# Neighbourhood attention of the first block, two heads at a time on the two halves of TensorE's array

## The chip, the cores and the metric

The kernel runs on one core of one Trainium2 chip. The metric is the device time of one execution in microseconds (us). All data is float32. The engines are called by the names of the profile: PE is TensorE's matmul, PEld its weight load, DVE is VectorE, ACT is ScalarE, POOL is GpSimd, SP is SyncE, which issues the loads of the weights.

## What is computed

The reference is a model of two blocks with two layers each, over 256 tokens of 1,024 features. The change touches one part of the first block, its neighbourhood attention. In each of the two layers it takes 8 heads of 64 features:

```python
mix-in of a layer of the first block (cut):
    proj = h @ w_in[i] + b_in[i]
    qkv = proj[..., 2 * CONV_CH:].reshape(B, T, 3, N_HEADS, HEAD_DIM)
    conv_out = conformer_conv(a, g, conv_w[i], ...)
    attn_out = neighbourhood_attention(q, k, v, rpb[i])   # softmax(q k / 8 + bias + window mask) v
    mix = jnp.concatenate([conv_out, attn_out], axis=-1) @ w_out[i] + b_out[i]
```

The kernel computes the scores of a head over all 256 keys; what lies outside the window is masked by the table `relb`, which holds the relative bias and the mask together.

## The kernel before

Every engine has a program of its own, written out by hand, and waits on semaphores. In layer `l` of the first block PE does, in this order: the projection, three units of `conditions(l)`, the norm of the convolution, the attention, the output product `block1_out`, and then the feed-forward part. In layer 0 the attention lies at 117 to 160 us of the span, in layer 1 at 567 to 611 us.

**The filler.** `conditions(l)` computes a product that only the second block needs. It is a generator of 13 units, numbered from 0. Unit u of PE multiplies one weight tile (`row`, 16 matmul instructions in four column quarters of 32) into bank 1, and then folds the row of unit u-1 (`fold`, 4 instructions of two columns). Unit 12 only folds. ACT has a generator of its own, which copies bank 1 to `cond_row` (L1088), one copy for each unit. Bank 1 is single: PE's `fill` lets row u start only when ACT has copied row u-1. Three units are done ahead of the norm; the attention asks for the rest, one at the head of each of its rounds, on PE and on ACT.

**The attention.** One head to a round, over `i`, as a pipeline. In round i

- PE does a filler unit; the scores of head i, into bank 2 or 3 (two products of 64 rows by 128 columns, four instructions); the transposes of head i-2 (four, L485), which wait for `nbr_prob`; and the product with v of head i-3 (two products with 64 output columns, four instructions), which waits for `nbr_turned`.
- ACT does a filler copy; the copy of the transposed head i-3 (L1124); the two exponentials of head i (L1130), which wait for `nbr_max`; and in every second round the copy of a finished pair of heads to `mix1` (L1136).
- DVE normalises head i-2 (reciprocal L1474, two multiplications L1476), and then adds the bias to the scores of head i (L1485) and takes the negated row maximum (L1488).

Probabilities have three buffers (`prob1[:, i % 3]`), their transposes two (`pt1`). All matmuls issued through the helper `mm` have line L377.

The loads of weights are issued by SP into a ring of six slots, each as soon as the unit that held the slot has been used. POOL loads `relb` for layer 1 when the last scores of layer 0 have been read (`nbr_scored`).

Of the kernel before, what the change touches and what calls it, by code (L numbers as in the profile page):

```python
# [8 lines left out]
ALU = mybir.AluOpType  # L9
ACT = mybir.ActivationFunctionType  # L10
AX = mybir.AxisListType


P = 128
T = 256
TT = T // P
# [4 lines left out]
CC = CONV_CH // P  # L21
# [137 lines left out]
def build(nc, weights, params, consts, x_t, ctx_t, p_t, rel, out):  # L159
    with ExitStack() as ctx:  # L160
# [14 lines left out]
        def carver(space, limit):  # L175
            at = [0]

            def carve(*shape):
                n = int(np.prod(shape))
                v = space[:, at[0]:at[0] + n]  # L180
                at[0] += n
                assert at[0] <= limit, at[0]
                names = "abcd"[:len(shape)]
                if len(shape) > 1:
                    v = v.rearrange(f"p ({' '.join(names)}) -> p {' '.join(names)}",
                                    **{k: s for k, s in zip(names[1:], shape[1:])})
                return v
            return carve
# [12 lines left out]
        gi, gf, lf, labs = cut(4, 8), cut(4, 8), cut(4, 8), cut(4, 8)  # L201


        cut = carver(work, WORK)
        cen, sq = cut(KC, T), cut(KC, T)
        res, mix1, ple = cut(KC, T), cut(KC, T), cut(KC, T)
# [8 lines left out]
        std1, rstd1, sig_sb = cut(T), cut(T), cut(2, T)  # L215
        cond_s = cut(KC, 32)

        gcmp, geq = (act_sb[:, i, 0, 0:TT * 64].rearrange("p (a b) -> p a b", b=64) for i in range(2))


        MIX, GLU, PROB, TAIL = 6144, 12288, 21624, 29048
        extra = [work[:, at:at + UC] for at in (0, UC, MIX, GLU, GLU + UC, PROB)]

        def slot_view(slot):
# [125 lines left out]
        def _(eng):  # L350
# [5 lines left out]
            def fill(key, bank, read_by):  # L356

                if readers[bank] is not None:
                    eng.wait_ge(*readers[bank])
                count[bank] += 1  # L360
                placed[key] = (bank, count[bank])
                readers[bank] = read_by
                return ps[:, bank, :]
# [12 lines left out]
            def mm(o, lhs, rhs, start, stop, **kw):  # L376
                ins = eng.matmul(o, lhs, rhs, start=start, stop=stop, **kw)  # L377
                if release[0]:
                    ins.then_inc(s["weights_used"], int(release[0]))
                    release[0] = 0  # L380
                return ins
# [84 lines left out]
            def block1_attention(l, filler):  # L466
                eng.wait_ge(s["qk_out"], CC * (l + 1))
                eng.wait_ge(s["v_out"], 2 * (l + 1))
                for i in range(HEADS + 3):
                    next(filler, None)  # L470
                    if i < HEADS:
                        b, p0 = 2 + i % 2, DH * (i % 2)
                        o = fill(("s", l, i), b, (s["nbr_scored"], HEADS * l + i + 1))
                        for t in range(TT):
                            last = mm(o[:, t * T:(t + 1) * T], q1[p0:p0 + DH, i // 2, t * P:t * P + P],
                                      k1[p0:p0 + DH, i // 2, :], True, True)
                        last.then_inc(bank_full[b], 1)
                    if 2 <= i < HEADS + 2:
                        h = i - 2
                        b = 4 + h % 2  # L480
                        eng.wait_ge(s["nbr_prob"], HEADS * l + h + 1)
                        o = fill(("pt", l, h), b, (s["nbr_turned"], HEADS * l + h + 1))
                        for t in range(TT):
                            for kt in range(TT):
                                last = eng.transpose(o[:, kt * T + t * P:kt * T + t * P + P],  # L485
                                                     prob1[:, h % 3, t, kt * P:kt * P + P], ident)
                        last.then_inc(bank_full[b], 1)
                    if i >= 3:
                        h = i - 3
                        eng.wait_ge(s["nbr_turned"], HEADS * l + h + 1)  # L490
                        if h % 2 == 0:
                            o2 = fill(("o", l, h // 2), 6 + (h // 2) % 2, (s["nbr_out"], CC * l + h // 2 + 1))
                        for kt in range(TT):
                            last = mm(o2[DH * (h % 2):DH * (h % 2) + DH, 0:T],
                                      v1[:, kt, h * DH:h * DH + DH], pt1[:, h % 2, kt, :], kt == 0, kt == TT - 1)
                        if h % 2 == 1:
                            last.then_inc(bank_full[6 + (h // 2) % 2], 1)

            def block1_out(l):
                eng.wait_ge(s["conv_mixed"], CC * (l + 1))  # L500
# [517 lines left out]
        def tile(eng, *key):  # L1018

            b, n = placed[key]  # L1020
            eng.wait_ge(bank_full[b], n)
            return ps[:, b, :]
# [28 lines left out]
        @block.gpsimd  # L1051
        def _(eng):

            eng.wait_ge(s["late_loaded"], 16 * N_LATE)
            for l in range(DEPTH):
                if l:
                    eng.wait_ge(s["nbr_scored"], HEADS * l)
                for r in range(ROWS):
                    p0 = GRID_W * (r % 2)
                    src = rel[l, :, :, ROWS - 1 - r:2 * ROWS - 1 - r, :].rearrange("c h i j -> c h (i j)")  # L1060
                    eng.dma_start(relb[p0:p0 + GRID_W, r // 2, :, :], src).then_inc(s["rel_loaded"], 16)
                eng.wait_ge(s["rel_loaded"], 16 * ROWS * (l + 1))
                for t in range(TT):
                    mask = con[:, CN("nbr_mask", t * T, T)].unsqueeze(1).broadcast_to([P, HEADS, T])
                    eng.tensor_tensor(relb[:, t], relb[:, t], mask, ALU.add).then_inc(s["rel_ready"], 1)
# [3 lines left out]
        def _(eng):  # L1069
# [47 lines left out]
                                   scale=par[:, PC(f"conv_ln_g{l}", j)]).then_inc(s["conv_mixed"], 1)  # L1117

            def block1_attention(l, filler):
                for i in range(HEADS + 4):  # L1120
                    next(filler, None)
                    if 3 <= i < HEADS + 3:
                        o = tile(eng, "pt", l, i - 3)
                        eng.activation(pt1[:, (i - 3) % 2].rearrange("p a b -> p (a b)"), o, ACT.Copy)\  # L1124
                            .then_inc(s["nbr_turned"], 1)
                    if i < HEADS:
                        k = HEADS * l + i + 1
                        eng.wait_ge(s["nbr_max"], k)
                        for t in range(TT):
                            eng.activation(prob1[:, i % 3, t, :], prob1[:, i % 3, t, :], ACT.Exp,  # L1130
                                           bias=rmax[:, i % 3, t:t + 1], accum_out=rsum[:, i % 3, t:t + 1])\
                                .then_inc(s["nbr_exp"], 1)
                    if i >= 5 and i % 2 == 1:
                        h2 = (i - 5) // 2
                        o = tile(eng, "o", l, h2)
                        eng.activation(mix1[:, CC + h2, :], o[:, 0:T], ACT.Copy).then_inc(s["nbr_out"], 1)  # L1136

            def block1_out(l):
                for c in range(KC):
# [240 lines left out]
        def _(eng):  # L1380
            order = [0]

            def link(ins):

                order[0] += 1
                ins.then_inc(s["dve_order"], 1)
                eng.wait_ge(s["dve_order"], order[0])
# [79 lines left out]

            def block1_attention(l):
                eng.wait_ge(s["rel_ready"], TT * (l + 1))
                for i in range(HEADS + 2):  # L1470
                    if i >= 2:
                        h = i - 2
                        eng.wait_ge(s["nbr_exp"], 2 * (HEADS * l + h + 1))
                        link(eng.reciprocal(rinv[:, h % 3, :], rsum[:, h % 3, :]))  # L1474
                        for t in range(TT):
                            ins = eng.tensor_scalar(prob1[:, h % 3, t, :], prob1[:, h % 3, t, :],  # L1476
                                                    rinv[:, h % 3, t:t + 1], None, ALU.mult)
                        ins.then_inc(s["nbr_prob"], 1)
                    if i < HEADS:
                        k = HEADS * l + i + 1  # L1480
                        pr = prob1[:, i % 3]
                        o = tile(eng, "s", l, i)
                        if i >= 3:
                            tile(eng, "pt", l, i - 3)
                        eng.tensor_tensor(pr, o.rearrange("p (a b) -> p a b", b=T), relb[:, :, i, :], ALU.add)\  # L1485
                            .then_inc(s["nbr_scored"], 1)
                        eng.wait_ge(s["nbr_scored"], k)
                        eng.tensor_reduce(rmax[:, i % 3, :], pr, AX.X, ALU.max, negate=True).then_inc(s["nbr_max"], 1)  # L1488

            def block1_out(l):  # L1490
                for c in range(KC):
# [705 lines left out]
```

## Time and profile before

| | |
|---|---|
| median of 3 runs | 2448.18 us (2445.6 to 2450.01) |
| the profiled execution's own time | 2445.93 us |
| its span in the profile | 2444.1 us |
| PE busy | 2205.6 us, 90% of the span |
| DVE busy | 691.0 us, 28% |
| ACT busy | 369.2 us, 15% |
| mean granted clock of TensorE | 0.949 of full speed |

The span is the time from the first to the last instruction in the trace; the remaining 1.8 us lie around it. Busy shares are averages over the whole program, which has stages with quite different limits; the 40 slices of the page are 61 us each, so that the attention of layer 0 is spread over the second and the third of them.

### The profile page before, as it was taken

Reading aid. Unit: us, or ns where it says so; the run is one execution under the profiler, and the core shown is the slowest. Engines: PE = TensorE matmul, PEld = TensorE weight load, DVE = VectorE, ACT = ScalarE, POOL = GpSimd, SP = SyncE. Lnnn points to the kernel's source line nnn. Section 1 sums busy time; section 2 is a strip of 40 time slices with the busy share of each in tenths; the row PEclk is TensorE's granted clock in tenths of the full one; section 3 lists DMA queues with packets and bytes.
Section 4 is the critical chain, followed back from the end, with each engine's and each line's share of the span. In section 5 each row is a group of like instructions: output and inputs, shape, how many; then the busy total and the mean of one; then the engine's idle time right before and its main releaser. Section 6 shows DMA issues by size and latency. Waiting matters only on the chain.

```text
span 2444.1 us, 34578 instructions
## 1 busy us (share of the span) xinstructions
PE 2205.6 (90%) x14880; PEld 1533.5 (63%) x14880; DVE 691.0 (28%) x1680; ACT 369.2 (15%) x894; POOL 24.3 (1%) x16
## 2 busy tenths in 40 slices
PE   7799999998899999999999999889986778998766
PEld 6668888785776566666666666437464454486455
DVE  2932000265311111111111111224027663232754
ACT  1132000104210000000000000120124230112331
POOL 1010000000000000000000000000000000000000
PEclk9999999998899999999999999999998889998778
DMA  8463444245249999999999999602210001122000
GB/s 291 155 225 128 148 154 155 104 155 207 69 170 420 420 420 421 420 420 420 420 421 420 420 416 417 266 35 86 86 52 1 1 1 69 69 104 86 0 1 17
DMA packets 71930, 506.59 MB, mean 207 GB/s; under 512 B 7776, under 2 KB 9824, under 8 KB 11232
## 3 DMA queue, kind: packets, MB, share of 16 engines
q1 hardware_dynamic: 69296, 497.18, 51.3%
q0 software_dynamic: 1152, 4.19, 0.7%
q8 instruction: 120, 1.97, 0.3%
q10 hardware_dynamic: 1328, 2.97, 0.3%
q14 instruction: 34, 0.28, 0.0%
HBM read 503.27 MB, written 1.05 MB: 206 GB/s over the span
## 4 chain that ended last, share of the span: by engine, by line
PE 56%; DMA 10%; DVE 7%; ACT 2%; issue 1%; SPq 0%; DVEq 0%; ACTq 0%
PE ps L377 54%; DMA ring<-weights 9%; DMA work<-weights 1%; PE ps L931 1%; DVE small L1941 1%; ACT work L1278 1%; DVE work L1406 1%; DVE work L1936 1%; DVE work L1858 0%; PE ps L603 0%; DVE work L1811 0%; DVE work L1802 0%; DVE work L1410 0%; DVE work L1906 0%; DVE work L1844 0%
## 5 line engine op out<-in xcount | busy, mean ns | idle before, releaser
L377 PE MATMUL ps<-work 128*32 128x256 f32 (+6 forms) x5464 | 569.1, 398 | 52.0 <-DMA ring<-weights 15.3
L377 PE MATMUL ps<-work,ring 128*128 128x256 f32 (+1 forms) x2048 | 575.8, 442 | 25.8 <-DVE work L1722 12.1
L377 PE MATMUL ps<-xc,ring 128*128 128x256 f32 x2368 | 520.6, 381 | 8.2 <-DVE xc L1418 7.1
L377 PEld LDWEIGHTS ps<-work,ring 128*128 128x128 f32 x2048 | 391.3, 192 | 206.1 <-issue 150.3
L377 PEld LDWEIGHTS ps<-xc,ring 128*128 128x128 f32 x2368 | 450.8, 191 | 82.3 <-DMA ring<-weights 11.3
L377 PEld LDWEIGHTS ps<-work 128*32 128x32 f32 (+3 forms) x5464 | 325.9, 127 | 228.5 <-issue 135.1
L377 PE MATMUL ps<-ring,work 128*32 128x256 f32 (+3 forms) x3832 | 407.0, 437 | 8.5 <-ACT work L1088 6.5
L377 PEld LDWEIGHTS ps<-ring,work 128*32 128x32 f32 (+1 forms) x3832 | 224.2, 123 | 141.9 <-issue 91.1
L1612 DVE TENSOR_TENSOR work<-work,ps 128x256 f32<-128x256 f32 x42 | 17.7, 421 | 455.0 <-ACT work L1182 455.0
L377 PE MATMUL ps<-work,con 128*128 128x256 f32 (+1 forms) x278 | 95.6, 497 | 41.3 <-DVE work L1444 13.7
L1182 ACT ACTIVATE work<-ps 128x256 f32<-128x256 f32 x42 | 16.1, 384 | 638.1 <-PE ps L377 638.1
L377 PEld LDWEIGHTS ps<-work,con 128*128 128x128 f32 x278 | 58.5, 218 | 69.1 <-issue 55.4
L1444 DVE SCALAR_TENSOR_TENSOR work<-work,par 128x256 f32<-128x256 f32 x240 | 95.2, 478 | 0.0
L931 PE MATMUL ps<-con,work 128*128 128x128 f32 x160 | 32.8, 329 | 55.3 <-ACT work L1327 54.4
L1597 DVE TENSOR_TENSOR work<-ps,work 128x512 f32<-128x512 f32 x68 | 47.1, 692 | 99.2 <-PE ps L377 99.0
L931 PEld LDWEIGHTS ps<-con,work 128*128 128x128 f32 x160 | 20.2, 163 | 85.0 <-issue 57.3
L1693 DVE TENSOR_TENSOR work<-work,ps 128x256 f32<-128x256 f32 x22 | 9.3, 421 | 205.9 <-ACT work L1220 205.9
L1764 DVE TENSOR_TENSOR work<-ps,con 128x256 f32<-128x256 f32 x10 | 4.2, 424 | 190.1 <-PE ps L377 189.9
L1220 ACT ACTIVATE work<-ps 128x256 f32<-128x256 f32 x22 | 8.4, 384 | 207.7 <-PE ps L377 207.7
L1334 ACT ACTIVATE small<-par,small 128x1 f32<-128x1 f32 x48 | 14.1, 294 | 166.0 <-DVE small L1942 165.9
L1750 DVE SCALAR_TENSOR_TENSOR work<-work,par 128x512 f32<-128x512 f32 (+1 forms) x64 | 38.8, 680 | 0.0
L1626 DVE TENSOR_TENSOR work<-work 128x512 f32<-128x512 f32 x14 | 9.7, 692 | 98.9 <-ACT work L1188 98.9
(218 smaller groups left out, 1129.8 us busy)
## 6 DMA issues: line engine op xcount, KB each, us to landing
ring<-weights SPq DMA_DIRECT2D x303, 1024.0 KB, 17.5
work<-weights SPq DMA_DIRECT2D x168, 1024.0 KB, 22.0
work<-rel POOLq DMA_DIRECT2D x8, 512.0 KB, 11.4
con<-consts ACTq DMA_DIRECT2D x1, 1368.0 KB, 10.2
xc<-x_t SPq DMA_DIRECT2D x1, 1024.0 KB, 7.5
xc<-ctx_t ACTq DMA_DIRECT2D x1, 1024.0 KB, 21.5
out<-work SPq DMA_DIRECT2D x1, 1024.0 KB, 3.9
par<-params SPq DMA_DIRECT2D x1, 872.0 KB, 9.0
```

Of the source, the lines that this page charges most:

```text
L377: ins = eng.matmul(o, lhs, rhs, start=start, stop=stop, **kw)
L931: last = eng.transpose(o[:, kt * P:kt * P + P], prob2[:, k % 4, kt * P:kt * P + P], ident)
L1182: eng.activation(pair_s[:, n % 2, :], o[:, 0:GW], ACT.Silu).then_inc(s["pair_silu"], 1)
L1278: ins = eng.activation(decay[:, n, :], amask[:, n, :], ACT.Exp, bias=nm_row[:, n:n + 1])
L1334: eng.activation(esink[:, k % 4, :], par[:, PC(f"sink{l}", h)], ACT.Exp, bias=rmax[:, k % 4, 0:1])
L1406: link(eng.reciprocal(rstd[:, 0:n], std[:, 0:n]))
L1444: ins = eng.scalar_tensor_tensor(out=conv_acc[:, j, :], in0=src, scalar=w, in1=conv_acc[:, j, :], op0=ALU.mult, op1=ALU.add)
L1597: return eng.tensor_tensor(r, o.rearrange("p (a b) -> p a b", b=T), r, ALU.add)
L1612: eng.tensor_tensor(pair_a[:, n % 2, :], pair_s[:, n % 2, :], o[:, GW:2 * GW], ALU.mult)\
L1750: ins = eng.scalar_tensor_tensor(out=acc, in0=src, scalar=w, in1=acc, op0=ALU.mult, op1=ALU.add)
L1936: eng.tensor_tensor(pr, o, con[:, CN("win_mask", qt * 2 * T, 2 * T)], ALU.add)\
L1941: link(eng.tensor_reduce(rmax[:, k % 4, 0:1], pr, AX.X, ALU.max, negate=True))
```

## The change

The attention goes over pairs of heads, `CC` = 4 rounds of scores in place of 8. A head of the pair has rows 0 to 63 of the array and the other rows 64 to 127 in the scores, which go to banks 2 and 3 and are issued in turns; in the product with v the two heads have columns 0 to 63 and 64 to 127, and are issued in turns too. Round i of PE is now: a filler unit, the transposes of pair i-2, the scores of pair i, another filler unit, the product with v of pair i-3. ACT's round: a filler copy, the copies of the transposed pair i-2, four exponentials, another filler copy, the copy of a finished pair to `mix1`. DVE normalises pair i-1 (one reciprocal of 4 columns, four multiplications) and then does one addition and one maximum over 1,024 columns for pair i. Probabilities have two buffers of a pair, transposes as well; the latter lie over `act_sb` and `silu_sb`, which the feed-forward part uses.

```diff
+        prob_pairs = work[:, PROB:PROB + 4 * TT * T].rearrange("p (a b c) -> p a b c", b=TT, c=T)
+        turned_pairs = work[:, ACT_AT:ACT_AT + 4 * TT * T].rearrange("p (a b c) -> p a b c", b=TT, c=T)
...
-                for i in range(HEADS + 3):
+                for i in range(CC + 3):
                     next(filler, None)
...
+                    if 2 <= i < CC + 2:
+                        k = CC * l + i - 1
+                        eng.wait_ge(s["nbr_prob"], k)
+                        for half in range(2):
+                            o = fill(("pt", l, i - 2, half), 4 + half, (s["nbr_turned"], 2 * k - 1 + half))
+                            for t in range(TT):
+                                for kt in range(TT):
+                                    last = eng.transpose(o[:, kt * T + t * P:kt * T + t * P + P],
+                                                         prob_pairs[:, 2 * (i % 2) + half, t, kt * P:kt * P + P], ident)
+                            last.then_inc(bank_full[4 + half], 1)
+                    if i < CC:
+                        both = [fill(("s", l, i, half), 2 + half, (s["nbr_scored"], CC * l + i + 1)) for half in range(2)]
                         for t in range(TT):
...
+                            for half in range(2):
+                                p0 = DH * half
+                                last = mm(both[half][:, t * T:(t + 1) * T], q1[p0:p0 + DH, i, t * P:t * P + P],
+                                          k1[p0:p0 + DH, i, :], True, True)
+                                if t == TT - 1:
+                                    last.then_inc(bank_full[2 + half], 1)
+                    next(filler, None)
                     if i >= 3:
...
+                        c = i - 3
+                        eng.wait_ge(s["nbr_turned"], 2 * (CC * l + c + 1))
+                        o2 = fill(("o", l, c), 6 + c % 2, (s["nbr_out"], CC * l + c + 1))
                         for kt in range(TT):
...
+                            for half in range(2):
+                                h = 2 * c + half
+                                last = mm(o2[DH * half:DH * half + DH, 0:T], v1[:, kt, h * DH:h * DH + DH],
+                                          turned_pairs[:, 2 * (c % 2) + half, kt, :], kt == 0, kt == TT - 1)
+                        last.then_inc(bank_full[6 + c % 2], 1)
...
             def block1_attention(l, filler):
-                for i in range(HEADS + 4):
+                for i in range(CC + 4):
                     next(filler, None)
...
+                    if 2 <= i < CC + 2:
+                        for half in range(2):
+                            o = tile(eng, "pt", l, i - 2, half)
+                            eng.activation(turned_pairs[:, 2 * (i % 2) + half].rearrange("p a b -> p (a b)"), o, ACT.Copy)\
+                                .then_inc(s["nbr_turned"], 1)
+                    if i < CC:
+                        eng.wait_ge(s["nbr_max"], CC * l + i + 1)
+                        for half in range(2):
+                            n = 2 * (i % 2) + half
+                            for t in range(TT):
+                                eng.activation(prob_pairs[:, n, t, :], prob_pairs[:, n, t, :], ACT.Exp,
+                                               bias=rmax[:, n, t:t + 1], accum_out=rsum[:, n, t:t + 1])\
+                                    .then_inc(s["nbr_exp"], 1)
+                    next(filler, None)
+                    if i >= 4:
+                        o = tile(eng, "o", l, i - 4)
+                        eng.activation(mix1[:, CC + i - 4, :], o[:, 0:T], ACT.Copy).then_inc(s["nbr_out"], 1)
...
+                for i in range(CC + 1):
+                    if i >= 1:
...
+                        eng.wait_ge(s["nbr_exp"], 4 * k)
+                        link(eng.reciprocal(rinv[:, slots, :], rsum[:, slots, :]))
+                        for n in range(slots.start, slots.stop):
+                            for t in range(TT):
+                                ins = eng.tensor_scalar(prob_pairs[:, n, t, :], prob_pairs[:, n, t, :],
+                                                        rinv[:, n, t:t + 1], None, ALU.mult)
                         ins.then_inc(s["nbr_prob"], 1)
...
+                        eng.tensor_tensor(pr, ps[:, 2:4, :].rearrange("p a (b c) -> p a b c", c=T),
+                                          relb[:, :, 2 * i:2 * i + 2, :].rearrange("p b a c -> p a b c"), ALU.add)\
                             .then_inc(s["nbr_scored"], 1)
                         eng.wait_ge(s["nbr_scored"], k)
...
+                        eng.tensor_reduce(rmax[:, slots, :], pr, AX.X, ALU.max, negate=True).then_inc(s["nbr_max"], 1)
```

## Rows read from the trace of the kernel before

**Rows 1.** The page: span, busy share and granted clock in 40 slices

```profile
span 2444.1 us, 34578 instructions
...
PE   7799999998899999999999999889986778998766
...
PEclk9999999998899999999999999999998889998778
```

**Rows 2.** Windows of the two attention stages, layer 0 and layer 1

```profile
core 0: us, PE busy (x) PEld busy (x) DVE busy (x) ACT busy (x) POOL busy (x), PEclk, DMA share, GB/s
116.87:160.28 43.41, 40.05 (x281) 23.55 (x280) 19.96 (x46) 22.42 (x61) 2.76 (x4) 0.88 0.66 226
566.92:611.19 44.27, 41.31 (x282) 24.08 (x281) 19.92 (x46) 22.16 (x60) 0.00 (x0) 0.84 0.57 214
```

**Rows 3.** Timeline of PE, layer 1, one head's round: start, us, instructions

```profile
587.91 1.07 PE L377 MATMUL ps<-ring,work 128*32 128x256 f32 x16
588.91 0.61 PE L377 MATMUL ps<-con,work 128*128 128x2 f32 x4
589.45 1.13 PE L377 MATMUL ps<-work 64*128 64x256 f32 x4
590.50 0.66 PE L485 MATMUL ps<-con,work 128*128 128x128 f32 x4
591.09 1.08 PE L377 MATMUL ps<-work 128*64 128x256 f32 x4
592.10 1.07 PE L377 MATMUL ps<-ring,work 128*32 128x256 f32 x16
```

**Rows 4.** Timeline of PE near the start of both stages, with waits

```profile
122.38 1.07 PE L377 MATMUL ps<-ring,work 128*32 128x256 f32 x16 [2.85 <-ACT work L1088]
...
572.26 1.94 PE L377 MATMUL ps<-ring,work 128*32 128x256 f32 x16 [2.41 <-ACT work L1088]
...
575.08 2.07 PE L377 MATMUL ps<-work 64*128 64x256 f32 x4
577.08 1.93 PE L377 MATMUL ps<-ring,work 128*32 128x256 f32 x16
...
581.88 1.12 PE L485 MATMUL ps<-con,work 128*128 128x128 f32 x4
582.93 1.86 PE L377 MATMUL ps<-ring,work 128*32 128x256 f32 x16
```

**Rows 5.** Timeline of ACT, start of the stage in layer 1

```profile
571.76 0.36 ACT L1088 ACTIVATE work<-ps 128x256 f32<-128x256 f32 x1
572.14 1.28 ACT L1130 ACT_TABLE_LOAD   x1
573.43 0.51 ACT L1130 ACTIVATE work<-work,small 128x256 f32<-128x256 f32 x1
...
573.94 0.49 ACT L1130 ACTIVATE work<-work,small 128x256 f32<-128x256 f32 x1
...
574.43 0.36 ACT L1088 ACTIVATE work<-ps 128x256 f32<-128x256 f32 x1
```

**Rows 6.** Timeline of DVE, layer 1

```profile
570.67 0.69 DVE L1485 TENSOR_TENSOR work<-ps,work 128x512 f32<-128x512 f32 x1
...
590.61 0.69 DVE L1485 TENSOR_TENSOR work<-ps,work 128x512 f32<-128x512 f32 x1 [2.05 <-PE ps L377]
591.34 0.69 DVE L1488 TENSOR_REDUCE small<-work 128x2 f32<-128x512 f32 x1
...
592.13 0.62 DVE L1476 TENSOR_SCALAR work<-work,small 128x256 f32<-128x256 f32 x2
```

**Rows 7.** Groups by shape, DVE: busy us, mean ns

```profile
L1802 DVE TENSOR_REDUCE work<-ps 128x8 f32<-128x1024 f32 x8 | 9.8, 1225 | 13.2 <-PE ps L377 13.2
```

**Rows 8.** Windows around changes of the granted clock, columns as in rows 2

```profile
122.10:123.80 1.70, 1.42 (x20) 0.92 (x20) 0.09 (x1) 1.67 (x3) 0.00 (x0) 1.00 0.00 0
123.80:125.50 1.70, 1.70 (x6) 1.33 (x5) 0.00 (x0) 1.11 (x5) 0.00 (x0) 0.50 0.69 212
132.30:134.00 1.70, 1.70 (x18) 0.66 (x10) 0.70 (x4) 1.25 (x5) 0.00 (x0) 0.50 0.17 19
570.10:571.80 1.70, 0.00 (x0) 0.00 (x0) 1.67 (x4) 1.70 (x5) 0.00 (x0) 0.75 1.06 443
583.70:585.40 1.70, 1.70 (x17) 0.86 (x10) 0.43 (x2) 1.36 (x6) 0.00 (x0) 0.74 0.21 63
```

**Rows 9.** Timeline of PE, last products with v in both layers

```profile
157.96 1.83 PE L377 MATMUL ps<-work 128*64 128x256 f32 x8
...
608.84 1.83 PE L377 MATMUL ps<-work 128*64 128x256 f32 x8
```

More of the change, by code:

```diff
@@ L201, in build @@
         gi, gf, lf, labs = cut(4, 8), cut(4, 8), cut(4, 8), cut(4, 8)
+        MIX, GLU, PROB, ACT_AT, TAIL = 6144, 12288, 21624, 25208, 29048
         cut = carver(work, WORK)
@@ L216, in build @@
         cond_s = cut(KC, 32)
+        prob_pairs = work[:, PROB:PROB + 4 * TT * T].rearrange("p (a b c) -> p a b c", b=TT, c=T)
+        turned_pairs = work[:, ACT_AT:ACT_AT + 4 * TT * T].rearrange("p (a b c) -> p a b c", b=TT, c=T)
         gcmp, geq = (act_sb[:, i, 0, 0:TT * 64].rearrange("p (a b) -> p a b", b=64) for i in range(2))
-        MIX, GLU, PROB, TAIL = 6144, 12288, 21624, 29048
         extra = [work[:, at:at + UC] for at in (0, UC, MIX, GLU, GLU + UC, PROB)]
@@ L468, in block1_attention @@
                 eng.wait_ge(s["v_out"], 2 * (l + 1))
-                for i in range(HEADS + 3):
+                for i in range(CC + 3):
                     next(filler, None)
-                    if i < HEADS:
-                        b, p0 = 2 + i % 2, DH * (i % 2)
-                        o = fill(("s", l, i), b, (s["nbr_scored"], HEADS * l + i + 1))
-                        for t in range(TT):
[L475 to L487, printed above, removed]
@@ L488, in block1_attention @@
+                    next(filler, None)
                     if i >= 3:
[L489 to L492, printed above, removed]
+                        c = i - 3
+                        eng.wait_ge(s["nbr_turned"], 2 * (CC * l + c + 1))
+                        o2 = fill(("o", l, c), 6 + c % 2, (s["nbr_out"], CC * l + c + 1))
@@ L493, in block1_attention @@
                         for kt in range(TT):
[L494 to L497, printed above, removed]
+                            for half in range(2):
+                                h = 2 * c + half
+                                last = mm(o2[DH * half:DH * half + DH, 0:T], v1[:, kt, h * DH:h * DH + DH],
+                                          turned_pairs[:, 2 * (c % 2) + half, kt, :], kt == 0, kt == TT - 1)
@@ L1056, in _ @@
                 if l:
-                    eng.wait_ge(s["nbr_scored"], HEADS * l)
+                    eng.wait_ge(s["nbr_scored"], CC * l)
                 for r in range(ROWS):
@@ L1119, in block1_attention @@
             def block1_attention(l, filler):
-                for i in range(HEADS + 4):
+                for i in range(CC + 4):
                     next(filler, None)
[L1122 to L1136, printed above, removed]
+                    if 2 <= i < CC + 2:
[15 more added lines that the diff above has]
+                        eng.activation(mix1[:, CC + i - 4, :], o[:, 0:T], ACT.Copy).then_inc(s["nbr_out"], 1)
             def block1_out(l):
@@ L1469, in block1_attention @@
                 eng.wait_ge(s["rel_ready"], TT * (l + 1))
[L1470 to L1477, printed above, removed]
-                        ins.then_inc(s["nbr_prob"], 1)
[L1479 to L1485, printed above, removed]
+                for i in range(CC + 1):
+                    if i >= 1:
+                        k = CC * l + i
+                        slots = slice(2 * ((i - 1) % 2), 2 * ((i - 1) % 2) + 2)
+                        eng.wait_ge(s["nbr_exp"], 4 * k)
[4 more added lines that the diff above has]
+                                                        rinv[:, n, t:t + 1], None, ALU.mult)
+                        ins.then_inc(s["nbr_prob"], 1)
+                    if i < CC:
+                        k = CC * l + i + 1
+                        slots = slice(2 * (i % 2), 2 * (i % 2) + 2)
+                        pr = prob_pairs[:, slots]
+                        for half in range(2):
+                            tile(eng, "s", l, i, half)
+                            if i >= 2:
+                                tile(eng, "pt", l, i - 2, half)
+                        eng.tensor_tensor(pr, ps[:, 2:4, :].rearrange("p a (b c) -> p a b c", c=T),
+                                          relb[:, :, 2 * i:2 * i + 2, :].rearrange("p b a c -> p a b c"), ALU.add)\
@@ L1486, in block1_attention @@
                             .then_inc(s["nbr_scored"], 1)
                         eng.wait_ge(s["nbr_scored"], k)
-                        eng.tensor_reduce(rmax[:, i % 3, :], pr, AX.X, ALU.max, negate=True).then_inc(s["nbr_max"], 1)
+                        eng.tensor_reduce(rmax[:, slots, :], pr, AX.X, ALU.max, negate=True).then_inc(s["nbr_max"], 1)
             def block1_out(l):
```

## The prediction, made before the changed kernel was run

> **What bounds the kernel now.** I read the page first: PE is busy nine tenths of most slices at nine tenths of its clock [rows 1], so time is won or lost where PE's own sequence is longer or shorter. Then the windows of the two stages that the change touches: 43.4 and 44.3 us, PE busy in 40 and 41 of them, DVE in 20 and ACT in 22, the DMA engines at 0.66 and 0.57 [rows 2]. All that can move is inside 88 us of 2,444.
>
> Then PE's timeline. A head's round is one unbroken run of PE: row and fold 1.54 us (587.91 to 589.45), scores 1.05, transposes 0.59, product with v 1.01, together 4.19 [rows 3]. So here PE is the bound, in most rounds. What the reader should see besides is the exception at the start of both stages: PE stands 2.85 and 2.41 us before a row, released by ACT's filler copy L1088 [rows 4]. Bank 1 is single, so each row waits for the copy of the row before it. In the present order this copy stands at the head of ACT's round, ahead of the exponentials that depend on PE, and is early except at the start, where ACT is late with other work.
>
> Last the clock. It is 1.00 until 123.80 and 0.50 after it, until 134.0; in layer 1 it is 0.50 from about 571 to about 584.7 [rows 8]. Half is 1.2 GHz, full 2.4. Both falls come with or just after the standing time of rows 4; both returns come only after more than 10 us in which PE had nearly no gap. At half clock row and fold take 2.82 us (572.26 to 575.08), scores 2.00, four transposes 1.05 [rows 4].
>
> **What the change takes away.** Scores: eight instructions per pair, issued in turns on two row halves. No row here shows row halves at work; the nearest is the filler row, where instructions on four column quarters go 16 to 1.00 us, 62 ns each, against 252 ns each for the product with v, alone on its 64 columns [rows 3]. So quarters run side by side. By that row two halves do as well: scores of a pair 1.05 us in place of 2.10. Upper bound: no overlap, 2.10. Product with v: column halves, the same kind as the row: 1.0 in place of 2.0, upper bound 2.0. Transposes and fillers: as many as before. PE's work falls by 2.06 us for each of 8 pairs, 16.5 us in all.
>
> The Trainium skill (TensorE: Matmul & The Clock Gate, Part 3) says that matmuls on different row groups run concurrently; by it the lower value holds for the scores too, and the sum is the same.
>
> **What it adds.** DVE: addition and maximum over 1,024 columns. The nearest row is 1.225 us for a reduction of that width [rows 7]; two of the present size would be 1.38. I take 1.25 start to start. ACT: four exponentials in place of two; one with its accumulator read takes 0.51 start to start [rows 5], four 2.1. DVE's four multiplications are 1.2 (two are 0.62 [rows 6]) with a reciprocal before. None of this fills an engine: 4 us of DVE and about 4.5 of ACT in a round of 8.
>
> But one part of the order is new. ACT's second filler copy of round i stands **behind** the four exponentials of pair i, and PE's first row of round i+1 waits for that copy. The exponentials wait for the maximum, this for the addition, this for the scores of pair i, and these come on PE after the first filler and the transposes of the same round. That is a closed loop through PE, DVE and ACT, once per round. From the end of the scores: hand-over 0.05, addition 1.25, maximum 1.26 with its hand-over, exponentials 2.1, copy and hand-over to PE 0.6 (the copy starts at 571.76, the row at 572.26 [rows 4, 5], and I add 0.1). In all 5.26 us. In it PE has the second filler, 1.54, and in round 3 also the product with v, 1.0; then it stands for 3.7 us (2.7 in round 3). Queued behind it are transposes and scores of the next round, and so DVE's addition and ACT's exponentials.
>
> **The schedule at full clock.** Round 0 of layer 1: DVE can add at 570.67 as now [rows 6], maximum ready at 573.2, table loaded at 573.42 [rows 5], exponentials done 575.5, row 5 of the filler at 576.05, where it now starts at 577.08 [rows 4]. Round 1 (no transposes): 1.54 + 1.05 + 5.26 = 7.85. Rounds 2 and 3: 1.54 + 1.18 + 1.05 + 5.26 = 9.03 each; two heads now take 8.38. Round 4 to 6, no more exponentials: filler 1.54, transposes 1.18, last fold 0.54, product 1.0, transposes 1.18, then two copies of ACT, 1.35 with hand-over, beside the next product, last product 1.0: 7.8. Sum 33.7 after 576.05: 609.75, against 610.67 (608.84 + 1.83 [rows 9]). Layer 0, from 122.38 [rows 4] with the same 3.79 to the next row: 159.88, against 159.79 [rows 9]. Together -0.8 us: the 16.5 us of PE's work become standing time of PE, and nothing is won.
>
> **The clock.** At half clock round 1 has 1.28 more for the filler and 0.95 more for the scores, 2.2; rounds 2 and 3 have 0.92 more for eight transposes too, 3.15 each. That is 8.5 per layer. The loop through DVE and ACT does not shrink in return. In the present kernel gaps of 2.4 and 2.85 us, one in a stage, went with a fall [rows 4, 8]; now there are four of 2.7 to 3.7 us (at half clock 2.4, since the filler is longer), and the 9 to 12 us between two are about what the return has needed. In the last fifth of the kernel, where PE is busy 6 to 9 tenths, the clock is granted at 7 to 9 tenths [rows 1], so it is not always at half. I take four fifths of the 8.5: 6.8 per layer, 13.6 for both. Bounds: nothing, and 15 per layer if the last 7.4 us of PE's work are at half clock as well.
>
> The Trainium skill (the same page, "HAM oscillation — how this bites in real kernels") tells of a kernel whose matmul bursts, each followed by a wait, started at the low clock every time. By it all of the 8.5 holds and the result is 3.4 us later. No row here decides between them.
>
> **Sum.** 2445.93 - 0.8 + 13.6 = 2458.7 for an execution like the profiled one. The median of the runs is 2.25 us above that one, so I forecast a median of 2461 us. DMA has no part: SP's loads follow PE's rows, which come no faster; POOL's load of the table for layer 1 only waits for the last addition of layer 0, 400 us ahead of its use. What follows the stages shifts with them.
>
> **Rivals.**
> - *Clock stays full* in most rounds (the scores now fill all rows of the array, which may keep it up): 2448.2 - 0.8, up to 4 us more: 2447 to 2452. Against it: gaps longer than those after which it fell. 0.16.
> - *Halves don't overlap*: scores of a pair 2.10 and 4.0 instead of 1.05 and 2.0; on the path once in each of rounds 1 to 3, 3 to 6 us per layer, and three products with v in the tail, 3 us: 12 to 18 us more than the forecast, 2473 to 2479. For it: only column quarters are seen to overlap. 0.14.
> - *Faster, PE stays the bound*: if the second copy is there before PE has done its second filler and product. A pair would take 3.08 + 1.18 + 1.05 + 1.0 = 6.3 us, and the kernel 2448.2 - 16.5 = 2431.7. It decides at a loop under 2.54 us after the scores; the loop is 5.26, of which the exponentials alone are 2.1. Only a wait that the trace does not have as I read it can give this. 0.06.
>
> **How the numbers follow.** The forecast's own case (halves overlap, the copy is late, half clock in a good part of rounds 1 to 3; 2453 to 2470) has 0.64. A measurement tells about 0.2% (4.9 us) from no change. The range takes the full-clock rival's lower end and the whole of the no-overlap one: 2447 to 2480. Same: the full-clock case, 0.15; faster: 0.06 and a little, 0.07; slower: the rest, 0.78.
>
> **What the changed profile would show.** Eight score instructions in about 1.1 us at full clock and eight of the product with v in about 1.0; PE idle before the filler row released by ACT L1088's counterpart, four times per layer, 2.2 to 3.7 us each; addition and maximum at about 1.22 us; granted clock of the two stages' windows lower than 0.88 and 0.84. I am wrong if that idle time is not there, or if PE's clock is 1.00 through it.

## The result and the profile after

The changed kernel takes 2461.71 us (median of 5 runs, 2459.32 to 2470.59) against 2448.18 us; the ratio of the two is 1.0063, with a 95% interval of 1.005 to 1.0076. It is slower by 13.5 us. The forecast was 2461 us, its range 2447 to 2480.

The page of the changed kernel, span, busy share and granted clock in 40 slices, beside [rows 1]:

```profile
span 2457.8 us, 34554 instructions
...
PE   7789999997899999999999999989987778998766
...
PEclk9979999997899999999999999999997889999788
```

The third slice, where most of the attention of layer 0 lies, has fallen from 9 to 7 in the clock, and the tenth, ahead of and in that of layer 1, from 8 to 7. The windows of the two stages, from the first filler row to the first product of `block1_out`, beside [rows 2]:

```profile
core 0: us, PE busy (x) PEld busy (x) DVE busy (x) ACT busy (x) POOL busy (x), PEclk, DMA share, GB/s
116.83:169.11 52.28, 38.95 (x281) 24.13 (x281) 18.35 (x34) 22.51 (x61) 2.71 (x4) 0.71 0.65 206
574.30:626.58 52.28, 38.89 (x282) 24.16 (x281) 18.36 (x34) 22.51 (x61) 0.00 (x0) 0.71 0.52 181
```

Each stage is 52.28 us long, where it was 43.4 and 44.3, though PE is busy 1.1 and 2.4 us less in it; the granted clock is 0.71 in place of 0.88 and 0.84. Both together are 16.9 us longer; the span is 13.7 us longer, so some 3 us came back outside the two stages. One place is the norm ahead of the attention in layer 1, whose last eight products were at full clock this time (1.97 us in place of 3.75). The timeline of PE in layer 0, beside [rows 3, 4]:

```profile
122.33 1.07 PE L379 MATMUL ps<-ring,work 128*32 128x256 f32 x16 [2.83 <-ACT work L1093]
...
125.98 1.93 PE L379 MATMUL ps<-ring,work 128*32 128x256 f32 x16 [2.05 <-ACT work L1093]
...
128.79 2.08 PE L379 MATMUL ps<-work 64*128 64x256 f32 x8
...
136.01 1.93 PE L379 MATMUL ps<-ring,work 128*32 128x256 f32 x16 [2.33 <-ACT work L1093]
...
140.62 2.08 PE L379 MATMUL ps<-work 64*128 64x256 f32 x8
142.63 1.93 PE L379 MATMUL ps<-ring,work 128*32 128x256 f32 x16
...
147.94 1.93 PE L379 MATMUL ps<-ring,work 128*32 128x256 f32 x16 [2.84 <-ACT work L1093]
...
156.12 1.08 PE L379 MATMUL ps<-work 128*64 128x256 f32 x8
159.87 1.07 PE L379 MATMUL ps<-ring,work 128*32 128x256 f32 x16 [2.67 <-ACT work L1093]
...
169.11 3.26 PE L379 MATMUL ps<-work,ring 128*128 128x256 f32 x14 [0.52 <-issue]
```

Two things are to be seen. The two halves of the array do work side by side: eight score instructions take 2.0 us at half clock (140.62 to 142.63), as four did, and the eight of the product with v 1.08 at full. And PE stands before the first row of rounds 1 to 4, released by ACT's filler copy (L1093 here). The rounds begin at 125.98, 136.01, 147.94 and 159.87, so a pair takes 10.0 and 11.9 us where two heads took 8.4. The view of waits in this stage adds it up, with the wait of 2.83 us at 122.33, which the kernel before has as well (2.85):

```profile
PE ps L379 <- ACT work L1093: 12.7, 5, 2.8
```

Round 2's loop through DVE and ACT, in the two engines' timelines:

```profile
142.94 1.23 DVE L1496 TENSOR_TENSOR work<-ps,work 128x1024 f32<-128x1024 f32 x1 [5.96 <-PE ps L379]
144.20 1.22 DVE L1500 TENSOR_REDUCE small<-work 128x4 f32<-128x1024 f32 x1
```

```profile
145.45 0.51 ACT L1137 ACTIVATE work<-work,small 128x256 f32<-128x256 f32 x1 [4.13 <-DVE small L1500]
...
147.43 0.36 ACT L1093 ACTIVATE work<-ps 128x256 f32<-128x256 f32 x1
```

From 142.63, when PE goes on from the scores to its second row, to the next round's row at 147.94 are 5.31 us; the forecast had 5.26.

### The profile page after: what moved, and what is told of

It reads as the page before. It is cut to its first block, busy times and chain, and to the rows that moved or that the text cites. A ratio compares the mean times of both kernels' runs of the same rounds, so it can differ in the third digit from the quotient of the medians.

```text
span 2457.8 us, 34554 instructions
## 1 busy us (share of the span) xinstructions
PE 2205.0 (90%) x14880; PEld 1537.2 (63%) x14880; DVE 688.8 (28%) x1656; ACT 369.1 (15%) x894; POOL 24.0 (1%) x16
## 3 DMA queue, kind: packets, MB, share of 16 engines
q8 instruction: 120, 1.97, 0.3%
HBM read 503.27 MB, written 1.05 MB: 205 GB/s over the span
## 4 chain that ended last, share of the span: by engine, by line
PE 55%; DMA 10%; DVE 8%; ACT 2%; issue 1%; DVEq 0%; SPq 0%; ACTq 0%
PE ps L379 53%; DMA ring<-weights 9%; DMA work<-weights 1%; PE ps L936 1%; DVE small L1953 1%; ACT work L1285 1%; DVE work L1413 1%; DVE work L1948 1%; DVE work L1870 0%; PE ps L608 0%; DVE work L1823 0%; DVE work L1814 0%; DVE work L1417 0%; ACT work L1137 0%; DVE work L1882 0%
## 5 line engine op out<-in xcount | busy, mean ns | idle before, releaser
L379 PE MATMUL ps<-work 128*32 128x256 f32 (+6 forms) x5464 | 557.1, 401 | 49.8 <-DMA ring<-weights 14.7
L379 PEld LDWEIGHTS ps<-work 128*32 128x32 f32 (+3 forms) x5464 | 319.6, 128 | 224.8 <-issue 135.3
L936 PEld LDWEIGHTS ps<-con,work 128*128 128x128 f32 x160 | 19.9, 161 | 84.1 <-issue 59.4
L1762 DVE SCALAR_TENSOR_TENSOR work<-work,par 128x512 f32<-128x512 f32 (+1 forms) x64 | 38.8, 676 | 0.0
L379 PEld LDWEIGHTS ps<-con,work 128*128 128x128 f32 x208 | 30.3, 217 | 13.0 <-issue 13.0
```

Source lines behind the costliest of these rows:

```text
L936: last = eng.transpose(o[:, kt * P:kt * P + P], prob2[:, k % 4, kt * P:kt * P + P], ident)
L1762: ins = eng.scalar_tensor_tensor(out=acc, in0=src, scalar=w, in1=acc, op0=ALU.mult, op1=ALU.add)
```

## Experiments

Each kernel was timed beside the kernel before, in three groups. The kernel before took 2449.43 us beside copy_ahead, old_late_copy, kept_busy and one_head_after_other, 2447.15 beside old_kept_busy, turned_behind, first_copy_ahead_too and next_max_first, and 2451.63 beside both_and_busy. Medians of different groups are compared only where the difference is far larger than that.

### The second copy ahead of the exponentials, and the kernel before with a late copy

copy_ahead, in ACT's `block1_attention` of the changed kernel:

```diff
+                    next(filler, None)
                     if i < CC:
                         eng.wait_ge(s["nbr_max"], CC * l + i + 1)
...
                                     .then_inc(s["nbr_exp"], 1)
-                    next(filler, None)
```

old_late_copy, in ACT's `block1_attention` of the kernel before:

```diff
                 for i in range(HEADS + 4):
-                    next(filler, None)
...
                                 .then_inc(s["nbr_exp"], 1)
+                    next(filler, None)
```

> ACT's second filler copy of a round is put ahead of the four exponentials; nothing else differs from the changed kernel. If the late copy is what costs (theory A), PE no longer stands before the first row of rounds 2 to 4, a pair's round is PE's own 6.3 us at full clock, and the kernel takes about 2434 us (2430 to 2440). If the loop of addition, maximum, exponentials and normalisation is itself too long for pairs (theory B), the standing times stay, only with another releaser, and the kernel stays above 2450 us.

> The kernel before, one head to a round, but ACT's filler copy of each round moved behind its two exponentials. Theory A: from the end of the scores 0.05 + 0.72 + 0.76 + 1.05 + 0.6 = 3.2 us to the next row, beside 1.6 us of PE's work, so PE stands for 1.6 us in each of 8 rounds of both layers, 25 us in all and some more by the clock: 2470 to 2490 us. Theory B: nothing changes, 2448 us.

Measured: copy_ahead 2423.29 us, ratio 0.9892 (0.9875 to 0.9908); old_late_copy 2485.54 us, ratio 1.0145 (1.012 to 1.017). One line's place makes the changed kernel 38 us faster and turns its loss of 13.5 us into a gain of 26; the same line late makes the kernel before 36 us slower. PE's timeline in copy_ahead, rounds 2 and 3 of layer 0, and its two stages in windows:

```profile
131.41 1.07 PE L379 MATMUL ps<-ring,work 128*32 128x256 f32 x16 [0.98 <-ACT work L1093]
...
135.53 1.13 PE L379 MATMUL ps<-work 64*128 64x256 f32 x8
137.29 1.07 PE L379 MATMUL ps<-ring,work 128*32 128x256 f32 x16 [0.62 <-ACT work L1093]
...
141.41 1.14 PE L379 MATMUL ps<-work 64*128 64x256 f32 x8
143.17 1.07 PE L379 MATMUL ps<-ring,work 128*32 128x256 f32 x16 [0.63 <-ACT work L1093]
```

```profile
120.75:154.32 33.57, 27.49 (x281) 17.63 (x281) 17.99 (x34) 21.58 (x60) 2.72 (x4) 0.99 0.87 297
560.92:594.50 33.58, 27.57 (x282) 17.64 (x281) 18.00 (x34) 21.58 (x60) 0.00 (x0) 0.99 0.76 282
```

A stage is 33.6 us in place of 52.3. The time is 11 us under the 2434 expected, and outside the range that went with it (2430 to 2440). A round is 5.88 us (131.41 to 137.29), not PE's 6.3, since rounds 1 and 2 have no product with v and eight transposes take 1.0 us and not 1.18; and the expectation counted nothing for the clock, which is 0.99 in this trace, also where it was at half in the kernel before. The 5.88 us are the loop named as theory B (DVE's additions start at 132.29 and 138.18, as far apart): it is there, but only 0.6 us per round longer than PE's own work. PE now stands for these 0.6 us before the second row of a round. That row waits for the copy at the head of ACT's round, which is queued behind the exponentials of the pair before.

Two cautions belong to this trace. The profiled execution was the slowest of its four (2429.83 us), and its two stages are only 20.5 us shorter than in the kernel before (87.68 against 67.15), where the medians differ by 26; no trace here shows where the rest lies. And the full clock at the start of its stages is not there whenever the copy is ahead: in the traces of one_head_after_other and turned_behind below it was at half there in both layers.

In old_late_copy PE's timeline has the new wait in the old form. In layer 0 PE stands 4.8, 3.0 and 1.9 us before the first three rows of this kind, and at full clock 1.4 us where 1.6 were expected:

```profile
135.22 1.94 PE L377 MATMUL ps<-ring,work 128*32 128x256 f32 x16 [2.99 <-ACT work L1088]
...
156.61 1.07 PE L377 MATMUL ps<-ring,work 128*32 128x256 f32 x16 [1.39 <-ACT work L1088]
```

### PE kept at work where it stood, in both kernels

kept_busy, in PE's `block1_attention` of the changed kernel, behind the scores and behind the product with v (bank 0 beyond column 256 is read by nobody):

```diff
+                    if i == 0:
+                        for _ in range(5):
+                            mm(ps[:, 0, T:2 * T], ident, xc[:, 0, 0:T], True, True)
                     next(filler, None)
                     if i >= 3:
...
                         last.then_inc(bank_full[6 + c % 2], 1)
+                    if i < CC:
+                        for _ in range(7 if i < 3 else 5):
+                            mm(ps[:, 0, T:2 * T], ident, xc[:, 0, 0:T], True, True)
```

old_kept_busy, in PE's `block1_attention` of the kernel before:

```diff
                         last.then_inc(bank_full[b], 1)
+                    if i == 0:
+                        for _ in range(5):
+                            mm(ps[:, 0, T:2 * T], ident, xc[:, 0, 0:T], True, True)
                     if 2 <= i < HEADS + 2:
```

> The changed kernel with PE kept at work where it stands: products of the identity with x into an unused part of bank 0, 5 after the scores of round 0, 7 at the end of rounds 0 to 2 and 5 at the end of round 3, in both layers. The output is the same; the extra products are 0.43 us each at full clock. If the clock fell because PE stood (theory A), it stays at 1.00 through the stages, rounds take 8 to 9 us in place of 10 to 12, and the kernel comes back to 2446 to 2452 us though the late copy is still there. If it fell for another reason (the half-array products or the transposes), it stays at 0.50, the extra products come on top, and the time is 2470 us or more.

> The kernel before with five extra products (0.43 us each, output unused) on PE in round 0 of both layers, where PE stood for 2.4 and 2.9 us. If that standing time is why the clock was at half for 10 and 13 us behind it, the clock stays at full there and the time falls by about 5 us in each layer, to 2438 us (2436 to 2442). That is then the part of copy_ahead's 26 us that comes from the clock and not from the paired products. If the half-array scores, filler folds and rows bring it down by themselves, 2449 us as before.

Measured: kept_busy 2443.56 us, ratio 0.9976 (0.9963 to 0.999); old_kept_busy 2437.45 us, ratio 0.9959 (0.9945 to 0.9973). Work whose result nobody reads makes both kernels faster. old_kept_busy met its expectation of 2438 us; kept_busy came out below its range of 2446 to 2452. Windows of kept_busy (layer 0) and of old_kept_busy (both layers):

```profile
115.89:159.20 43.31, 40.84 (x344) 28.41 (x343) 18.36 (x34) 22.20 (x61) 2.71 (x4) 1.00 0.73 239
```

```profile
120.20:159.03 38.83, 37.78 (x292) 23.24 (x291) 19.97 (x46) 22.28 (x61) 2.77 (x4) 1.00 0.74 253
564.91:603.73 38.82, 37.79 (x291) 23.23 (x291) 19.92 (x46) 22.28 (x61) 0.00 (x0) 1.00 0.67 244
```

The granted clock is 1.00 throughout. The rounds of kept_busy, in PE's timeline:

```profile
126.07 1.07 PE L379 MATMUL ps<-ring,work 128*32 128x256 f32 x16
...
133.88 1.07 PE L379 MATMUL ps<-ring,work 128*32 128x256 f32 x16 [0.47 <-ACT work L1099]
...
142.72 1.07 PE L379 MATMUL ps<-ring,work 128*32 128x256 f32 x16 [0.57 <-ACT work L1099]
...
151.57 1.07 PE L379 MATMUL ps<-ring,work 128*32 128x256 f32 x16 [0.34 <-ACT work L1099]
```

7.81, 8.84 and 8.85 us: the schedule at full clock of the prediction had 7.85, 9.03 and 9.03. So of the changed kernel's stage of 52.3 us, 9.0 go when the clock is held up (52.28 - 43.31), and 9.7 more with the late copy (43.31 - 33.57). The medians say much the same: 18.2 us from the changed kernel to kept_busy, 20.3 from there to copy_ahead. And the kernel before had a loss by the clock itself, 4.6 and 5.5 us in its two stages (43.41 and 44.27 against 38.8). At full clock the changed order with its late copy is 4.5 us per stage longer than single heads (43.31 against 38.83; 1.0 of this is the extra products' own, as told below), and pairs with the copy ahead are 5.3 us shorter (33.57); that is what the paired halves bring, of the 8.2 us of PE's work that they save in a stage.

### The order in which the halves are issued

one_head_after_other, on top of copy_ahead, in PE's `block1_attention`, and the same with `kt` in the product with v:

```diff
-                        for t in range(TT):
-                            for half in range(2):
+                        for half in range(2):
+                            for t in range(TT):
```

> As copy_ahead, but within a pair all products of the first head are issued before those of the second, both in the scores and in the product with v. If two halves work side by side only when they are issued in turns, scores go back to 2.1 us and the product to 2.0 us per pair, 2.06 us more for 8 pairs: 16 us above copy_ahead, about 2450 us. If PE overlaps them from its queue in either order, the time is that of copy_ahead.

Measured: 2423.64 us, ratio 0.9892 (0.9875 to 0.9908), the time of copy_ahead. PE's timeline has the scores of pairs 0 and 2 at full clock:

```profile
121.66 1.14 PE L379 MATMUL ps<-work 64*128 64x256 f32 x8
...
137.58 1.14 PE L379 MATMUL ps<-work 64*128 64x256 f32 x8
```

Eight instructions in 1.07 us (137.58 to the next row at 138.65), with four of one head ahead of four of the other; eight of the product with v take 1.02 in the same way. The first of the two expectations was wrong: turns are not needed.

The trace shows something else besides. Nothing but the order within a pair differs from copy_ahead, and yet the clock fell at the start of both stages. PE's wait at the start of layer 0:

```profile
124.96 1.94 PE L379 MATMUL ps<-ring,work 128*32 128x256 f32 x16 [2.16 <-ACT work L1093]
```

The granted clock is 0.84 over the stage of layer 0 (119.61 to 155.14) and 0.90 over that of layer 1 (560.86 to 595.40). They are 35.5 and 34.5 us long, 2.0 and 1.0 more than in copy_ahead; the medians do not differ, and this profiled execution (2425.75 us) was even the faster one. So with the copy ahead a fall at the start costs 1 to 2 us of a stage.

### The place of the transposes

turned_behind, on top of copy_ahead, in PE's `block1_attention`; the block of the scores is moved whole:

```diff
+                    if i < CC:
+                        both = [fill(("s", l, i, half), 2 + half, (s["nbr_scored"], CC * l + i + 1)) for half in range(2)]
...
                     if 2 <= i < CC + 2:
                         k = CC * l + i - 1
...
-                    if i < CC:
-                        both = [fill(("s", l, i, half), 2 + half, (s["nbr_scored"], CC * l + i + 1)) for half in range(2)]
```

> As copy_ahead, but on PE the transposes of pair i-2 stand behind the scores of pair i, as in the kernel before, in place of ahead of them. DVE's addition of pair i still waits for these transposes, since probabilities have two buffers. In copy_ahead a pair's round is 5.88 us, which is DVE's and ACT's loop (addition, maximum, exponentials, normalisation); the scores are done 0.7 to 3 us before DVE takes them. So the order of the two on PE should be worth nothing: 2423 us, within 3. If the transposes' place is a gain of its own, the time rises by 1 us for each of four rounds or more: 2427 and above.

Measured: 2423.16 us, ratio 0.9902 (0.9885 to 0.9918), as expected. With the copy ahead, the order in which probabilities are turned and scores are made is worth nothing that can be measured here. The clock fell at the start of both stages in this trace too (0.90 over each of them, which are 34.5 us long).

### What is left: the first copy, and DVE's order

first_copy_ahead_too, on top of copy_ahead, on ACT:

```diff
                 norm(f"conv{l}", CC, T)
+                next(filler)
                 conv_silu(l)
...
                 for i in range(CC + 4):
-                    next(filler, None)
+                    if i:
+                        next(filler, None)
```

next_max_first, on top of that, in DVE's `block1_attention`; the block of addition and maximum is moved whole:

```diff
                 for i in range(CC + 1):
+                    if i < CC:
+                        k = CC * l + i + 1
...
                     if i >= 1:
                         k = CC * l + i
...
-                    if i < CC:
-                        k = CC * l + i + 1
```

both_and_busy, on top of first_copy_ahead_too, on PE, at the end of round 0:

```diff
+                    if i == 0:
+                        for _ in range(2):
+                            mm(ps[:, 0, T:2 * T], ident, xc[:, 0, 0:T], True, True)
```

> As copy_ahead, and ACT's first filler copy in the attention is put ahead of the four SILUs of the convolution. The 2.3 us for which PE stands before row 4 go; PE then waits for the next copy, about 1.4 us, since ACT is still in the SILUs. From then on DVE's and ACT's loop sets the pace, and begins about 1.4 us earlier: 2420 us (2416 to 2423). If the standing time before row 4 is only moved, 2423.

> As first_copy_ahead_too, and DVE does the addition and the maximum of pair i before it normalises pair i-1. The loop through DVE and ACT then has no normalisation in it (1.3 us less), and PE's own 5.3 to 6.3 us bound the round: 0.6 us less in each of three rounds of both layers, 3 to 4 us less than first_copy_ahead_too, about 2417 us. If something else holds the round at 5.9 us, no difference.

> As first_copy_ahead_too, with two extra products of 0.43 us on PE (output unused) at the end of round 0 of both layers, where PE still stood for 1.1 to 1.3 us and the clock was at half for the scores of pair 1 and most of the row behind them, some 1.5 us per layer. If that gap is what lets the clock fall, the time is 2 to 3 us less, about 2418 us; if not, 2421. Either is at the edge of what three rounds tell, so the trace decides: granted clock 1.00 or 0.50 in the scores of pair 1.

Measured: first_copy_ahead_too 2420.99 us, ratio 0.9888 (0.9871 to 0.9904); next_max_first 2420.47, ratio 0.9887 (0.9871 to 0.9904); both_and_busy 2421.4, ratio 0.9877 (0.9859 to 0.9894). The intervals of all three overlap each other and that of copy_ahead, so by the times none of the three is shown to gain anything over it, and the 2420 expected of the first cannot be told from the 2423 of its alternative. By its trace first_copy_ahead_too has stages of 31.9 and 32.1 us, 1.6 less than copy_ahead, and the 2.4 and 2.3 us of standing before row 4 are gone; 1.14 and 1.30 us before row 5 have come in their place.

next_max_first gained nothing, and PE's timeline shows why:

```profile
139.41 1.09 PE L480 MATMUL ps<-con,work 128*128 128x128 f32 x8 [1.21 <-DVE work L1500]
```

DVE now normalises pair 1 (L1500 there) only when it has done the addition and the maximum of pair 2, which wait for scores from PE; the transposes wait for the normalisation, and the next scores are queued behind the transposes. The wait has only changed its releaser.

both_and_busy was to tell whether a gap of 1.1 us lets the clock fall. In first_copy_ahead_too PE's timeline had

```profile
124.90 1.07 PE L379 MATMUL ps<-ring,work 128*32 128x256 f32 x16 [1.14 <-ACT work L1093]
...
126.51 2.08 PE L379 MATMUL ps<-work 64*128 64x256 f32 x8
```

and with the two products the same scores are at full clock in both layers, 1.1 us in place of 2.1:

```profile
127.74 1.14 PE L379 MATMUL ps<-work 64*128 64x256 f32 x8
...
564.88 1.13 PE L379 MATMUL ps<-work 64*128 64x256 f32 x8
```

The time did not follow: the scores are earlier, and DVE takes them no earlier, since it waits for ACT's exponentials. That the gap was the cause is likely, but a fall and its absence in one profile each, two stages in each, do not show it.

## Why the prediction was right, step by step

- **The closed loop through ACT's second copy**: shown. PE stands four times per layer for 2.0 to 2.9 us (2.2 to 3.7 were forecast), and moving the copy takes the loss away (copy_ahead) or makes one (old_late_copy). The loop is 5.31 us against 5.26.
- **PE's work**: right, and the upper bounds fell away. Row halves and column halves overlap; a pair's scores take 1.07 us, its product with v 1.02, the lower bounds. What the prediction took from a row on column quarters held for row halves too. The Trainium skill (TensorE: Matmul & The Clock Gate, Part 3) says that matmuls on different parts of the array run concurrently, and this trace agrees.
- **DVE and ACT**: addition 1.23 and maximum 1.22 us, four exponentials 2.0, as taken (1.25, 1.26 and 2.1, with hand-overs).
- **The schedule at full clock**: 7.85, 9.03, 9.03 forecast, 7.81, 8.84, 8.85 measured where the clock is held up. The last part, to the end of the last product with v, was taken at 7.8 and is 7.1 (151.57 to 158.68).
- **The clock**: the right mechanism, its size a little low. It stood as four fifths of 8.5 us per layer, 6.8. The rounds of the changed kernel are 10.03, 11.93 and 11.93, 8.0 us above the schedule and 8.4 above those of kept_busy; the last part, begun at full clock and then at half for some 3.4 us (161.5 to 164.9), is 8.7 against 7.1. That is 10.0 us per layer where 6.8 were taken. (The stage of kept_busy is only 9.0 shorter, since its products delay the row of round 1 by 1.0.) In the kernel of which the Trainium skill tells (the same page, "HAM oscillation — how this bites in real kernels"), each burst behind a wait started at the low clock; taken over to this kernel, that sets the 8.5 in full. The trace agrees for the gaps after rounds 0, 1 and 2, though at the second the clock had been at half before it (0.50 from 124.0 to 144.2). It does not agree for the one after round 3, behind which the row runs at full clock (159.87), nor for the first gap of the stage (122.33).
- **The sum**: the stages are 8.9 and 8.0 us longer, 16.9 together, where 12.8 were forecast. The median came out within 1 us of the forecast because some 3 us came back outside the stages, for which the prediction had no term. The mechanism was right; that closeness is luck, as the five runs spread over 11 us.
- **The rivals**: that the halves do not overlap is out; that the clock stays full is out; that PE stays the bound needs another order, and with it the kernel is at 2423, below the 2431.7 given. In copy_ahead's trace the half clock at the start of the stages is gone as well; but one_head_after_other and turned_behind have it and take the same time, so this does not account for the difference, which stays open.

## What to carry to other kernels

When work is merged into longer rounds, look for small steps that keep their place in the program of an in-order engine: a copy that frees a single buffer, once ahead of the long instructions and now behind them, closed a loop over three engines and cost, with the clock that fell in its waits, more than the merged products gained. Find it by asking of each wait what stands queued ahead of its releaser. And where the matmul engine stands for a few microseconds and then works at half its clock, price the two apart; products of no use in the gap do that in one run.

## What the hardware did that was not expected

- Two heads on row halves overlap fully with all four instructions of one head issued ahead of the other's: 1.07 us for eight (one_head_after_other) against 1.05 us for four of a single head.
- Matmuls whose result nobody reads make a kernel faster: five products in each of two stages, 4.9 us of PE's time in all (2.43 in a stage), took 10 us off the kernel before.
- The length of a gap alone does not tell whether the clock falls. Behind 2.83 us it fell to 0.50 in the changed kernel, some 1.6 us after the end of the gap, and behind only 2.16 us it was at 0.50 at once in one_head_after_other; behind 2.39 and 2.32 us it stayed at full in copy_ahead in both layers; behind 1.14 and 1.30 us in first_copy_ahead_too it fell, for the scores and most of a row. What decides is open.
